# Third and last layer's up projection: from the fifth pair of tiles on, seven products of sums of two by two blocks in place of eight

## What is computed

```python
def swiglu_ffn(x, norm_g, w13, w2):
    g, u = jnp.split(rms_norm_2(x, norm_g) @ w13, 2, axis=-1)
    return (jax.nn.silu(g) * u) @ w2
```

## Time and profile before

| | |
|---|---|
| median of 3 runs | 2789.34 us (2785.57 to 2793.76) |
| span of the profiled execution | 2788.5 us |
| PE busy | 2714.7 us (97%) |
| PE weight loads busy | 2149.0 us (77%) |
| DVE busy | 1521.6 us (55%) |
| ACT busy | 1050.5 us (38%) |
| POOL busy | 787.1 us (28%) |
| HBM traffic | 78 GB/s over the span |

### The profile page before, as it was taken

The page is one execution under the profiler, slowest core; times in us unless marked ns, Lnnn a source line. Parts: engine busy times, 40 slices in busy tenths (PEclk is TensorE's granted clock), DMA queues, the critical chain, the costliest instruction groups (busy, mean ns, idle before and its releaser), DMA issues. The chain is left out here.

```text
span 2788.5 us, 37901 instructions
## 1 busy us (share of the span) xinstructions
PE 2714.7 (97%) x13902; PEld 2149.0 (77%) x13902; DVE 1521.6 (55%) x1931; ACT 1050.5 (38%) x1869; POOL 787.1 (28%) x715
## 2 busy tenths in 40 slices
PE   8999999899999999999999999999999999999999
PEld 6888888656798788888777765788888756888887
DVE  4477763464756676764567665544434266644422
ACT  5433332434345433333345545322222358322221
POOL 3231111350834431112102655311112054311100
PEclk9999999999999999999999999999999999999999
DMA  4222223311100022233222121323233200222233
GB/s 154 76 97 93 96 91 95 111 53 53 61 2 20 31 98 93 95 92 96 92 78 76 37 61 33 98 91 98 98 89 100 91 31 1 76 98 98 96 89 102
DMA packets 80541, 218.98 MB, mean 79 GB/s; under 512 B 21917, under 2 KB 22045, under 8 KB 80158
## 3 DMA queue, kind: packets, MB, share of 16 engines
q1 hardware_dynamic: 79262, 215.17, 24.5%
q10 hardware_dynamic: 1152, 2.10, 0.2%
HBM read 215.14 MB, written 2.10 MB: 78 GB/s over the span
## 5 line engine op out<-in xcount | busy, mean ns | idle before, releaser
L312 PE MATMUL psum<-rounded,high_r 128*128 128x512 f32 x3040 | 1200.5, 395 | 30.4 <-DVE rounded L400 10.3
L316 PE MATMUL psum<-rounded,ring_low 128*128 128x512 f32 x3040 | 1187.1, 391 | 0.0
L314 PE MATMUL psum<-rounded,high_r 128*128 128x512 f32 x3040 | 1187.0, 390 | 0.0
L337 ACT ACTIVATE high_r<-ring 128x1024 fp32r<-128x1024 f32 (+2 forms) x432 | 420.4, 973 | 1378.6 <-PE psum L316 1354.2
L342 DVE TENSOR_TENSOR ring_low<-ring,high_r 128x1024 fp32r<-128x1024 f32 (+2 forms) x432 | 524.9, 1215 | 539.2 <-ACT high_r L337 537.8
L312 PEld LDWEIGHTS psum<-rounded,high_r 128*128 128x128 f32 x3040 | 572.9, 188 | 183.4 <-issue 35.4
L316 PEld LDWEIGHTS psum<-rounded,ring_low 128*128 128x128 f32 x3040 | 572.8, 188 | 120.9
L314 PEld LDWEIGHTS psum<-rounded,high_r 128*128 128x128 f32 x3040 | 573.4, 189 | 118.0 <-issue 1.7
L786 DVE TENSOR_TENSOR arena<-psum,inverse 128x512 f32<-128x512 f32 x176 | 121.5, 691 | 314.5 <-PE psum L316 314.3
L639 POOL CAST rounded<-rows 128x512 f32 (+1 forms) x88 | 53.8, 611 | 785.8 <-DVE rows L791 785.8
L435 POOL TENSOR_TENSOR arena<-resid 128x512 f32<-128x512 f32 x41 | 52.3, 1276 | 237.9 <-DVE resid L423 237.9
(11 more groups left out here) (419 smaller groups left out, 2859.6 us busy)
## 6 DMA issues: line engine op xcount, KB each, us to landing
ring<-in_up SPq DMA_DIRECT2D x176, 512.0 KB, 3.4
ring<-in_down SPq DMA_DIRECT2D x64, 384.0 KB, 3.1
ring<-in_down SPq DMA_DIRECT2D x64, 320.0 KB, 2.9
ring<-in_even_in SPq DMA_DIRECT2D x36, 512.0 KB, 3.3
ring<-in_sgu_in SPq DMA_DIRECT2D x16, 512.0 KB, 3.6
ring<-in_even_out SPq DMA_DIRECT2D x16, 384.0 KB, 3.1
ring<-in_qkv SPq DMA_DIRECT2D x12, 512.0 KB, 3.3
ring<-in_sgu_out SPq DMA_DIRECT2D x8, 512.0 KB, 3.4
```

What stands on the lines that cost most here:

```text
L312: nc.tensor.matmul(psum[:, m, :], high_r[:, r % HIGHS, blk], x_high, start=(k0 + k == 0), stop=False)
L314: nc.tensor.matmul(psum[:, m, :], high_r[:, r % HIGHS, blk], x_low, start=False, stop=False)
L316: mm = nc.tensor.matmul(psum[:, m, :], ring_low[:, r % R, blk], x_high, start=False, stop=end)
L337: nc.scalar.activation(high_r[:, r % HIGHS, 0:nk * P], ring[:, r % R, 0:nk * P], ACT.Copy).then_inc(unit_high, 1)
```

## The change

Layers three and four get a function of their own, `feed_forward_of_seven`. The first four pairs (`PLAIN` = 8 units) go as before. Each later pair is seen as a two by two block product: two output tiles (gate, value), two halves of the 1024 input features, two halves of 256 tokens. Seven products of sums replace the eight block products (Strassen's scheme in Winograd's form):

- Activations. They are now normalized first (8 `normalize`), and four sums and differences of their quarters are made, once per layer (`differ` on DVE, `later_differences` on POOL). That gives seven operands of 128 x 1024, each split into high and low.
- Weights. For each pair POOL makes three sums of 128x512 (`add`) and DVE a fourth (`add_fourth`). The seven factors of 128x512 are rounded by ACT (`high`) and split by DVE (`low`), one by one.
- Products. A product is 4 blocks by three matmuls of 128x128 weights and 128x256 activations: 12 matmuls. A pair is 84 matmuls of 256 columns, where it was 48 of 512. Products 0, 2, 4 and 6 add up in one bank, 1 and 5 in a second, 3 stands in a third. Between them ACT copies what a bank holds (`keep`, three per pair, ahead of products 2 and 4), and DVE adds (`add_up`, three per pair, after products 3, 4 and 5; product 6 waits for the second).
- Results. The two scales of a pair by the inverse root fall away; the multiply by the gate is in two halves of 256 tokens. The hidden tiles are left whole in `arena` and are split only around the end of the stage (`hidden` on ACT and DVE for tiles 2 to 13, 20 and 21, POOL for the others), because the operands occupy their place till then.
- Counting. `unit_done`, `unit_high` and `unit_low` count 7 per pair in place of 2; `st.count` takes the place of `st.first` in every wait for them.
- Loading. Still two units per pair; the first slot of a pair is reloaded after product 3, the second after product 6.

The core of the diff (indentation halved):

```diff
+IN_SEVEN = ("up2", "up3")
+PLAIN, SEVEN = 8, 7
...
+  n_counts += PLAIN + (of_name - PLAIN) // 2 * SEVEN if name in IN_SEVEN else of_name
...
+  n = g * st.body + (st.count + r)
...
+def feed_forward_of_seven(layer, out_name, out_rhs, out_inputs, out_ready=None, out_bank_free=None):
...
+  def operand(n):
+    both = flat(early_sets[:, 4 * n:4 * n + 4, :] if n < 5 else later_sets[:, 4 * (n - 5):4 * (n - 5) + 4, :])
+    return both[:, 0:2 * T], both[:, 2 * T:4 * T]
...
+  operand_of = [normed(0, 0), difference(0), difference(1), normed(4, 0), difference(2), normed(4, 1), difference(3)]
+  def combined_sum(h, n):
+    at = 3 * h + n
+    return (work[:, at, :], work_low[:, at, :]) if at < 4 else (rows[:, at - 2, :], rows_low[:, at - 2, :])
+  def raw(h, row, part):
+    cols = slice(part * T, (part + 1) * T)
+    return ring[:, 2 * h + row, cols], ring_low[:, 2 * h + row, cols]
+  def factor(h, q):
+    return [raw(h, 0, 0), raw(h, 1, 0), combined_sum(h, 1), raw(h, 0, 1), combined_sum(h, 0), combined_sum(h, 2), raw(h, 1, 1)][q]
+  def high_slot(q):
+    return high_r[:, q // 2, q % 2 * T:(q % 2 + 1) * T] if q < 4 else more_high[:, q - 4, :]
...
+  def item(g, h, q):
+    return g * (2 * SEVEN) + (start_of + SEVEN * h + q + 1)
...
+      def body(g):
+        for h in range(2):
+          for row, q in ((0, 3), (1, 6)):
+            sp.wait_ge(unit_done, item(g, h, q))
+            load_unit(sp, st, g + (PLAIN // R + 1), 2 * h + row)
...
+      def product(g, h, q, to, opens):
+        pe.wait_ge(unit_low, item(g, h, q))
+        x_hi, x_lo = operand(q)
+        high, low = high_slot(q), factor(h, q)[1]
+        for k in range(4):
+          blk, ts = slice(k * P, (k + 1) * P), slice(k * HALF, (k + 1) * HALF)
+          nc.tensor.matmul(to, high[:, blk], x_hi[:, ts], start=(opens and k == 0), stop=False, skip_group_check=True)
+          nc.tensor.matmul(to, high[:, blk], x_lo[:, ts], start=False, stop=False, skip_group_check=True)
+          mm = nc.tensor.matmul(to, low[:, blk], x_hi[:, ts], start=False, stop=(k == 3), skip_group_check=True)
+        mm.then_inc(unit_done, 1)
...
+      def body(g):
+        for h in range(2):
+          starting = isinstance(g, int) and g == 0
+          a, b, c = (bank(h, n) for n in "abc")
...
+            pe.wait_ge(scaled, PLAIN - 1)
+            pe.wait_ge(x_low, 2)
+          if not starting:
+            pe.wait_ge(summed_up, g * 6 + (3 * h - 3))
+          product(g, h, 1, c, True)
+          pe.wait_ge(copied, g * 6 + (3 * h + 1))
+          if starting and h == 0:
+            pe.wait_ge(x_low, 3)
+          product(g, h, 2, a, False)
+          if starting and h == 0:
+            pe.wait_ge(scaled, PLAIN - 2)
+            pe.wait_ge(x_low_pool, 1)
+          product(g, h, 3, b, True)
+          pe.wait_ge(copied, g * 6 + (3 * h + 3))
+          if starting and h == 0:
+            pe.wait_ge(x_low, 4)
+          product(g, h, 4, a, False)
+          if starting and h == 0:
+            pe.wait_ge(x_low_pool, 2)
+          product(g, h, 5, c, False)
+          pe.wait_ge(summed_up, g * 6 + (3 * h + 2))
+          if starting and h == 0:
+            pe.wait_ge(x_low, 5)
+          product(g, h, 6, a, False)
+      loop(pe, groups, body)
...
+      def add(g, h):
...
+        s3, s2 = combined_sum(h, 0)[0], combined_sum(h, 1)[0]
+        nc.gpsimd.tensor_tensor(s3, a11, a21, ALU.subtract).then_inc(added, 1)
+        pool.wait_ge(added, g * 6 + (3 * h + 1))
+        nc.gpsimd.tensor_tensor(a21, a21, a22, ALU.add).then_inc(added, 1)
+        nc.gpsimd.tensor_tensor(s2, a22, s3, ALU.subtract).then_inc(added, 1)
+      pool.wait_ge(normed_done, KD)
+      pool.wait_ge(first_differences, 2)
+      nc.gpsimd.tensor_tensor(difference(2), normed(4, 1), normed(0, 1), ALU.subtract).then_inc(later_differences, 1)
...
+          act.wait_ge(added, g * 6 + (3 * h + {4: 1, 1: 2, 2: 3}[q]))
+        if isinstance(g, int) and g == 0 and h == 0:
+          act.wait_ge(unit_done, start_of - (1 if q < 2 else 0))
+        else:
+          act.wait_ge(unit_done, g * (2 * SEVEN) + (start_of + SEVEN * (h - 1) + q + 1))
+        nc.scalar.activation(high_slot(q), factor(h, q)[0], ACT.Copy).then_inc(unit_high, 1)
...
+      def keep(g, h, q):
+        act.wait_ge(unit_done, item(g, h, q))
+        source, to = {0: (bank(h, "a"), kept_at(h, 0)), 1: (bank(h, "c"), middle(h, 0)), 2: (bank(h, "a"), kept_at(h, 1))}[q]
...
+      def body(g):
...
+        for h in range(2):
+          done = ending and h == 1
+          if h:
+            gate(g, 0)
+          elif not starting:
+            gate(g - 1, 1)
+          high(g, h, 3)
+          if starting and h == 0:
+            operand_high(5)
+          for q in range(3):
+            keep(g, h, q)
+            high(g, h, 4 + q)
+            if starting and h == 0 and q == 0:
+              operand_high(6)
+            if done:
+              hidden(2 + q)
+          if done:
+            split_high(act, after, 0, 0)
+            hidden(5)
+            split_high(act, after, 0, 1)
+            for k in range(6, 9):
+              hidden(k)
+          else:
+            for q in range(3):
+              high(g if h == 0 else g + 1, 1 - h, q)
+      loop(act, groups, body)
+      gate(groups - 1, 1)
...
+      def normalize(k):
...
+      def add_fourth(g, h):
+        dve.wait_ge(added, g * 6 + (3 * h + 3))
+        nc.vector.tensor_tensor(combined_sum(h, 2)[0], raw(h, 0, 1)[0], combined_sum(h, 1)[0], ALU.subtract).then_inc(fourth_added, 1)
...
+      def low(g, h, q):
+        if q in (0, 4):
+          dve.wait_ge(added, g * 6 + (3 * h + (1 if q == 0 else 3)))
+        dve.wait_ge(unit_high, item(g, h, q))
+        full, rest = factor(h, q)
+        nc.vector.tensor_tensor(rest, full, high_slot(q).bitcast(F32), ALU.subtract).then_inc(unit_low, 1)
...
+      def add_up(g, h, n):
+        dve.wait_ge(unit_done, item(g, h, (3, 4, 5)[n]))
+        dve.wait_ge(copied, g * 6 + (3 * h + (1, 2, 3)[n]))
+        to, one, other = ((gate_at(h)[:, 0:HALF], bank(h, "b"), kept_at(h, 0)), (middle(h, 1), bank(h, "a"), middle(h, 0)),
...
+      def multiply(g, h):
+        dve.wait_ge(unit_done, item(g, h, 6))
+        dve.wait_ge(gated, g * 2 + (FIRST + h + 1))
+        dve.wait_ge(summed_up, g * 6 + (3 * h + 3))
+        to = home(g, h)
+        nc.vector.tensor_tensor(to[:, 0:HALF], bank(h, "a"), rows[:, h, 0:HALF], ALU.mult).then_inc(multiplied, 1)
+        nc.vector.tensor_tensor(to[:, HALF:T], middle(h, 1), rows[:, h, HALF:T], ALU.mult).then_inc(multiplied, 1)
...
+      add_low(dve, out_name, out_taken, out_inputs, handed)
+      for r in range(PLAIN):
+        if r + 2 < PLAIN:
+          split_low(dve, st, (r + 2) // R, (r + 2) % R)
+        if r == 0:
+          invert()
+        plain_scale(r)
+        if r % 2:
+          plain_multiply(r // 2)
+        if r < 2:
+          for k in range(4 * r, 4 * r + 4):
+            normalize(k)
+          differ(r)
+        if 2 <= r < 5:
+          operand_low(r - 1, r - 2)
+        if r == 6:
+          operand_low(5, 4)
+      for q in range(2):
...
+      def body(g):
...
+        for h in range(2):
+          done = ending and h == 1
+          low(g, h, 3)
+          if h:
+            multiply(g, 0)
+          elif not starting:
+            multiply(g - 1, 1)
+          low(g, h, 4)
+          if done:
+            hidden(2)
+          low(g, h, 5)
+          if done:
+            hidden(3)
+          low(g, h, 6)
+          if starting and h == 0:
+            operand_low(7, 6)
+          if done:
+            hidden(4)
+          for n in range(3):
+            add_up(g, h, n)
+            if done:
+              if n < 2:
+                split_low(dve, after, 0, n)
+              hidden(5 + n)
+            else:
+              if n == 2:
+                add_fourth(g if h == 0 else g + 1, 1 - h)
+              low(g if h == 0 else g + 1, 1 - h, n)
+      loop(dve, groups, body)
+      hidden(8)
```

277 lines of the change are left out of this document (260 added, 17 removed).

## The result

The changed kernel takes **2813.9 us** (median of 4 runs, 2812.7 to 2820.9) against 2789.8 us for the kernel before on the same chip: ratio 1.0093, 95% interval 1.0078 to 1.0108. It is slower by 0.9%, above the top of the range.

What follows compares the result with a forecast made beforehand. PE, busy for 97% of the span, was taken as the bound. Products -38.7, start +8.6, end +10.0 and clock +2.8 sum to -17.3 us, giving 2772 us as the median; range 2752 to 2796.

Steps and rivals of the forecast that it cites:

- Products: Seven products on PE: pitch between 0.1133 and 0.1200 us, middle 0.1167 taken, -38.7 us.
- rival 2: Products: excess belongs to 512 columns, nearly gone at 256; pitch 0.109, 2749 us; chance 0.02.
- The middle of the stage: Within pairs: DVE's work, 8.4 us with POOL's slowing, fits the pair's 9.8 us; costed at nothing.
- The start: Ahead of the first product: PE waits 1.3, 0.9 and 2.1 us for DVE, 4.3 per layer, +8.6 us.
- The end: Last product 6 is 3.1 us late, down projection's third unit 1.9; 5.0 us per layer, +10.0 us.
- The clock: After the 3.1 us stall at product 6 matmuls run at 1.2 GHz: 1.4 us per layer, +2.8 us.
- rival 3: Products: weight load not fully hidden, pitch 0.130, 2812 us; chance 0.13.
- Rival 4: Within pairs: DVE becomes the bound, slowed by 1.4 throughout; pair 10.2 instead of 9.8 us, 2786 us; chance 0.09.

Runs made afterwards that it cites:

- e_pitch: Kernel before, with the third layer's up projection in matmuls of 256 columns and the last layer's in matmuls of 128; span of the only execution 3034.0 us.
- e_order: Changed kernel, POOL's sums kept; on DVE the second `add_up` of each pair moved ahead of the next pair's first low part; 2798.3 us.
- e_start: Changed kernel with normalizations spread over three plain units, first factor's low part earlier, POOL's first two hidden tiles behind its first sums; 2816.8 us.
- e_first: Changed kernel with POOL's sums on DVE, e_start's spread normalizations, e_tail's end, first factors one plain unit earlier, POOL's two hidden tiles behind its last operand; 2776.6 us.
- e_sums: Changed kernel with POOL's three factor sums per pair computed by DVE, the next pair's first low part behind the second `add_up`; 2796.8 us.
- e_late: e_first with POOL starting its two hidden tiles only after the second pair, not right behind its last operand; 2770.5 us.
- e_tail: e_sums plus e_end, with DVE instead of POOL splitting hidden tiles 14 to 19 and two down projection splits put earlier; 2779.7 us.
- e_end: Changed kernel, last pairs only: high parts of down projection's first two units wait for products 2 and 3, second `add_up` before first unit's low part; 2815.7 us.

## Why the prediction was wrong

- **Products.** The mechanism held, the size was the worse end of the bracket: 0.119 (0.120 in e_pitch), not the middle of 0.1167. The term is -32, not -38.7 us: 7 of the 42 us by which the forecast missed. The excess belongs to the instruction. The middle was a guess between two ends that the rows did not part. The 0.109 of rival 2 is refuted. The section that the prediction cites for it, "Back-to-back issue gap" of the Trainium skill's page "TensorE: Matmul & The Clock Gate", calls that formula the gap of an isolated matmul, not that of a stream.
- **The middle of the stage, costed at nothing: the step that failed.** I took POOL's effect as a factor of 1.4 over 3.9 us and compared the sum of DVE's work, 8.4 us, with the pair's 9.8. Three things were off. DVE is *blocked* until POOL's operation ends (low parts 1.46 to 1.80 us in the pair shown and not 1.0); POOL's sums lasted 1.32 to 1.75 us and not 1.29, as they are held up too; and the total was the wrong thing to look at. PE waits for one position of DVE's queue. I had followed product 6's chain by product and copy, and not by what stands ahead of its `add_up` on DVE: the next pair's low part. Cost: about 16 us, as e_order shows. It is the largest single term. The start makes another 8 us of the 42, the end and the clock together 12 to 13 and the products 7; about 1 goes back by the untouched part and by the median's distance to the profiled span.
- **The start.** Waits of 1.3, 0.9 and 2.1 were forecast; there are three before plain units, 2.9 us together in the third layer and 3.2 in the last, and 4.1 before the first product: 7.2 in place of 4.3 per layer, and with slow restarts 8.3. The third comes from an operand's low part beside POOL's later differences, the same block again: 3.45 us (first row below), where alone it takes 1.22. Before the first product the multiply of unit 8 took 1.49 us and the two low parts behind it 2.35 beside POOL's first sums, in place of 0.69 and 1.29. That the work is also DVE's to do, and not only badly placed, is what e_start and e_first speak for: what was taken from the start came back among the products.
- **The end.** Product 6 waited 3.7 (forecast 3.1) and the third unit 2.0 (forecast 1.9), both at the named places. These terms held. What I didn't see is that they are not additive: removing the first alone won nothing, since DVE's hidden tiles came next.
- **The clock.** Forecast 1.4 us per layer. In the third layer 18 starts behind the 4.1 us wait and 10 behind the 3.7 us wait come about 0.21 us after the one before, 1.2 GHz. Six of 512 columns at 0.43 follow, and eight more behind the 2.0 us wait in the down projection. The granted clock was 0.58 from 2050 to 2056 us (second row below). Against 0.119 and 0.2266 these starts cost some 5.5 us in the third layer and 4.3 in the last. Behind the waits of 0.5 to 1.8 us within the pairs no such stretch follows. One stall was counted; there were three in the third layer and two in the last.
- **Rivals.** None happened as written. The time lies 2 us from rival 3's 2812, which is chance: it named that for a pitch of 0.130 that isn't there. Rival 4 named the right engine and neighbour but priced DVE's sum of work, 2786; e_sums runs without waits at the same 86%. A change whose break-even was a pitch of 0.122, with 0.120 as a bound, had 4 us of room per layer, and a probability of 0.14 for slower was too small for that.
- **Behind the products.** 5.2 us per layer on the mean. In the third layer the wait of 2.0 with its restart makes 2.3 and the two stretches at half clock 1.2 and 1.6; in the last layer 2.3, 0.9, and 0.9 at two late starts, one of them for a hidden tile.
- **Open.** The first pair's last 3.5 us in e_late were not tried further, nor were POOL's rest and the earlier splits of e_tail parted. About a third of the pairs of the changed kernel shows a wait; what decides which ones was not followed up.

The two rows named above, DVE's timeline and the window of the changed kernel:

```profile
1833.94 3.45 DVE L1199 TENSOR_TENSOR rounded<-arena,rounded 128x1024 fp32r<-128x1024 f32 x1 [1.65 <-ACT rounded L1080]
...
2050.00:2056.00 6.00, 3.56 (x14) 3.39 (x15) 2.39 (x3) 0.74 (x2) 5.76 (x7) 0.58 0.00 1
```

## What to carry to other kernels

When work is moved to POOL beside a DVE that reads two SBUF tiles, count each overlap as a full wait for POOL's operation, and ask which DVE instruction stands behind it in the queue that PE is waiting for. Check an in-order engine by position and due time, not by its sum: here a swap of two lines was worth as much as moving three operations to another engine. An edit that removes one wait should be tried together with the next one in line; two edits that won nothing alone (e_end, e_start) were, e_start with changes, part of the versions that beat both kernels.

## What the runs showed of the hardware

- Matmuls in the rounded type cost 0.012 to 0.013 us each over their stream at 512 and at 256 columns, with new 128 x 128 weights each; at 128 columns the pitch was 0.1115 us, where the stream is 0.053.
- A DVE subtraction of two SBUF tiles of 512 columns that started beside one of POOL's sums of two SBUF tiles ended 0.55 us after POOL's end, 102 times of 103; in the other order POOL's ended 1.14 to 1.18 us after DVE's and lasted 1.62 to 1.86 us in place of 1.31. A DVE sum with one input in PSUM kept its 0.41 us.
- With POOL out of the hidden tiles and two splits earlier (e_tail), and six tiles of 0.62 us more for DVE, the end got faster.
